# Squaring the recurrence's decay on VectorE instead of ScalarE, in a two-block layer stack

## The reference

```python
r = jax.nn.sigmoid(jnp.einsum('bsni,nij->bsnj', xb, w_a) + b_a).reshape(B, S, LRU_WIDTH)
i = jax.nn.sigmoid(jnp.einsum('bsni,nij->bsnj', xb, w_x) + b_x).reshape(B, S, LRU_WIDTH)
log_a = -LRU_C * r * jax.nn.softplus(-a_param)
a = jnp.where(reset, 0.0, jnp.exp(log_a))
mult = jnp.where(reset, 1.0, jnp.sqrt(-jnp.expm1(2.0 * log_a)))
b_in = xf * i * mult
_, h = lax.associative_scan(combine, (a, b_in), axis=1)      # h[t] = a[t] h[t-1] + b_in[t]
y = jax.nn.sigmoid(gate_a) * y_a + jax.nn.sigmoid(gate_b) * y_b
```

## Time and profile before

| What | Value |
|---|---|
| Median of three runs | 1880.51 us (1879.97 to 1885.79) |
| The profiled execution, its own time | 1880.51 us |
| Its span in the trace | 1878.7 us |
| TensorE busy | 1781.3 us, 95% of the span |
| VectorE, ScalarE, GpSimd busy | 976.1, 730.6 and 785.8 us |

### The profile page before, as it was taken

One profiled execution on the slowest core, in us unless ns is written; L12 is line 12 of the kernel. 1 busy time (PEld: TensorE's weight loads), 2 busy tenths in 40 slices (PEclk: granted clock), 3 DMA queues, 4 the chain that ended last, 5 costly groups with the idle time before them and its releaser, 6 DMA issues. The chain is left out here.

```text
span 1878.7 us, 23593 instructions
## 1 busy us (share of the span) xinstructions
PE 1781.3 (95%) x8447; PEld 1443.5 (77%) x8453; DVE 976.1 (52%) x1688; ACT 730.6 (39%) x1254; POOL 785.8 (42%) x363
## 2 busy tenths in 40 slices
PE   5987988999999999999999999999999999999997
PEld 4865867777888776878888888788776778888886
DVE  6989688748459977253324210559966131101112
ACT  4332365652357464232212222367554242222221
POOL 3345233325545520535445545355510544444442
PEclk9998999999999999999999999999999999999998
DMA  5433122206323310335555522233210222233311
GB/s 215 146 110 126 46 90 79 93 22 239 104 94 101 113 46 23 101 133 181 190 179 191 190 90 90 79 103 111 101 46 12 90 90 90 90 101 101 101 56 45
DMA packets 56057, 197.66 MB, mean 105 GB/s; under 512 B 6929, under 2 KB 7953, under 8 KB 55698
## 3 DMA queue, kind: packets, MB, share of 16 engines
q1 hardware_dynamic: 55954, 196.26, 31.0%
HBM read 194.14 MB, written 2.10 MB: 104 GB/s over the span
## 5 line engine op out<-in xcount | busy, mean ns | idle before, releaser
L458 POOL TENSOR_TENSOR WL<-RAW,WH 128x1024 fp32r<-128x1024 f32 x260 | 662.2, 2554 | 897.2 <-ACT WH L541 682.9
L1595 PE MATMUL bank<-HH,WH 128*128 128x512 f32 x1120 | 437.2, 390 | 6.6 <-POOLq L463 4.1
L1597 PE MATMUL bank<-HH,WL 128*128 128x512 f32 x1120 | 435.9, 389 | 0.0
L1596 PE MATMUL bank<-HL,WH 128*128 128x512 f32 x1120 | 435.8, 389 | 0.0
L541 ACT ACTIVATE WH<-RAW 128x1024 fp32r<-128x1024 f32 x260 | 271.3, 1051 | 261.0 <-PE bank L1597 235.0
L1595 PEld LDWEIGHTS bank<-HH,WH 128*128 128x128 f32 x1120 | 210.3, 188 | 52.7 <-issue 9.7
L1597 PEld LDWEIGHTS bank<-HH,WL 128*128 128x128 f32 x1120 | 210.3, 188 | 44.1
L1596 PEld LDWEIGHTS bank<-HL,WH 128*128 128x128 f32 x1120 | 210.3, 188 | 43.2
L1530 DVE TENSOR_TENSOR HF<-SILU,bank 128x512 f32<-128x512 f32 x44 | 30.3, 688 | 333.2 <-PE bank L1597 330.2
L1595 PE MATMUL bank<-HDH,WH 128*128 128x512 f32 x352 | 137.0, 389 | 0.0
L1597 PE MATMUL bank<-HDH,WL 128*128 128x512 f32 x352 | 136.9, 389 | 0.0
(11 more groups left out here) (336 smaller groups left out, 2943.3 us busy)
## 6 DMA issues: line engine op xcount, KB each, us to landing
RAW<-in_stream SPq DMA_DIRECT2D x364, 512.0 KB, 3.3
X<-in_xt SPq DMA_DIRECT2D x2, 1024.0 KB, 6.1
out_t<-YA SPq DMA_DIRECT2D x8, 256.0 KB, 2.2
ACC<-in_pos SPq DMA_DIRECT2D x1, 256.0 KB
gains<-in_gains SPq DMA_DIRECT2D x1, 224.0 KB
CS<-in_cs SPq DMA_DIRECT2D x1, 128.0 KB
cw<-in_cw SPq DMA_DIRECT2D x1, 128.0 KB
par<-in_par SPq DMA_DIRECT2D x1, 115.0 KB
```

The lines of the kernel that those rows point to most:

```text
L458: nc.gpsimd.tensor_tensor(lo(k)[:], raw(k)[:], hi(k)[:].bitcast(F32), ALU.subtract).then_inc(sem["passed"], mark("passed", *k))
L1595: nc.tensor.matmul(out, A[0], B[0], start=first, stop=False)
L1596: nc.tensor.matmul(out, A[0], B[1], start=False, stop=False)
L1597: return nc.tensor.matmul(out, A[1], B[0], start=False, stop=last)
```

## The change

Per layer, ScalarE's 8 Square instructions and their semaphore go. `one_aa(n)` on VectorE now waits for the Exp itself, multiplies LR[n] by itself into YT[n % 2], waits for that result, and then does the same (a^2 + 1) times YA as before, reading YT. The wait of the sigmoid of ga(4) for `one_aa(3)`, which protected SG[4] to SG[7], goes too. So does the tensor AA.

```diff
@@ -744,10 +739,6 @@
                         act.wait_ge(sem["tanh"], value("tanh", L, n))
                         nc.scalar.activation(LR[:, n, :], LR[:, n, :], ACT.Exp, scale=csc[:, L, n:n + 1]).then_inc(
                             sem["lru_a"], mark("lru_a", L, n))
-                    for n in ns:
-                        act.wait_ge(sem["lru_a"], value("lru_a", L, n))
-                        nc.scalar.activation(decay_square(n), LR[:, n, :], ACT.Square).then_inc(
-                            sem["lru_aa"], mark("lru_aa", L, n))
 
                 def roots(ns):
 
@@ -767,8 +758,6 @@
                             sem["xc_hi"], mark("xc_hi", L, n))
                     for n in GA_BESIDE[q]:
                         split_through(("ga", L, n))
-                        if n == 4:
-                            act.wait_ge(sem["one_aa"], value("one_aa", L, 3))
                         evict(SG[:, n, :], "ga", L, n, func=ACT.Sigmoid)
                     split_through(("lg", L, q))
                     for n in (2 * q, 2 * q + 1):
@@ -1415,8 +1404,10 @@
 
                 def one_aa(n):
 
-                    dve.wait_ge(sem["lru_aa"], value("lru_aa", L, n))
-                    V.scalar_tensor_tensor(out=YA[:, n, :], in0=decay_square(n), scalar=1.0, in1=YA[:, n, :],
+                    dve.wait_ge(sem["lru_a"], value("lru_a", L, n))
+                    V.tensor_tensor(YT[:, n % 2, :], LR[:, n, :], LR[:, n, :], ALU.mult).then_inc(step, 1)
+                    dve.wait_ge(step, own())
+                    V.scalar_tensor_tensor(out=YA[:, n, :], in0=YT[:, n % 2, :], scalar=1.0, in1=YA[:, n, :],
                                            op0=ALU.add, op1=ALU.mult).then_inc(
                         sem["one_aa"], mark("one_aa", L, n))
 
```

More of the change, by code:

```diff
@@ L166 @@
     "read_act", "full", "ca", "read_dve", "gmix", "h_hi", "lru_par", "lru_w", "topk", "iscore", "cos_sin",
-    "cmp_shift", "cmp_exp", "nmax", "mix_hi", "x_new", "conv", "xc_hi", "tanh", "lru_a", "lru_aa", "one_aa", "mult",
+    "cmp_shift", "cmp_exp", "nmax", "mix_hi", "x_new", "conv", "xc_hi", "tanh", "lru_a", "one_aa", "mult",
     "ya_gated", "c_hi", "y_full", "y_hi", "hid", "hid_hi", "x_half", "h_lo", "yb", "y_lo", "cmp_p", "xc_lo",
@@ L312, in program @@
         XCL = w("XCL", [P, 2, S], F32R, 84)
-        AA = w("AA", [P, 4, S], F32, 80)
         V2 = w("V2", [P, NT, D], F32, 32)
@@ L387, in spread @@
             return ap.rearrange(dims, o=1).broadcast_to(shape)
-        def decay_square(n):
-            return SG[:, 4 + n, :] if n < 4 else AA[:, n - 4, :]
         block = ctx.enter_context(nc.Block())
```

## The result

The changed kernel takes 1893.45 us, the median of seven runs (1890.62 to 1898.97). The kernel before takes 1883.12 us in the seven runs beside them (1879.97 to 1885.79). The ratio is 1.0057 with an interval of 1.0042 to 1.0073, so the change makes the kernel slower by 0.4 to 0.7%. The direction was predicted. The time lies 0.45 us above the end of the predicted range. The profiled execution took 1893.11 us. A ratio is worked out from all the runs of both kernels, and so it can differ by some hundredths of a per cent from the quotient of the two medians. Two runs in a slow state are in no median and no ratio of this document: one of the kernel before (7348.35 us) and one of e5_before_early (2393.78 us).

A forecast was written before the change was run, and what follows sets the result against it. TensorE, busy 95% of the span, was taken as the bound, with `one_aa(7)` delaying it one for one. 1880.5 + 5.8 (2 x 2.89, two layers) + 1.1 (one clock fall) = 1887.4 us, range 1881.9 to 1893.0.

The forecast's parts named there:

- the falls of the clock: TensorE's clock lowered behind the new stall at gb(3): 1.7 us gross, 1.1 net each, one counted for two layers.
- the starting time: Time of the kernel before that the sum starts from: 1880.5 us, the profiled execution and also the median.
- The pairs: Each added VectorE multiply, followed at once by the instruction needing its result: 0.71 us, 2.84 us for a group of four.
- the first group: Multiplies of tiles 0 to 3: covered by conv(5) starting 1.33 us early and a shorter XCL lock wait; 0.05 us left.
- What bounds the stage: Recurrence stage: what delays `one_aa(7)` delays TensorE at gb(3) one for one; making it earlier gives back only 0.2 us.
- the lock wait of XCL: XCL after conv(6), held by GpSimd's subtraction for 1.6 us before; it takes in 1.5 us of the first group's lateness.
- the cover: What hides the first four multiplies: 1.33 us gained at conv(5) and XCL's lock wait; without both, up to 2.84 us.
- the walk: Step-by-step timing of tiles 0 to 3 in the second layer, from the earlier copy to XCL after conv(6).
- The second group: Multiplies of tiles 4 to 7: full cost of 2.84 us; with 0.05 from the first group, gb(3) starts 2.89 us late.
- The twins above: Pauses near the end of attention in both layers: the second layer's clock fell to 0.57, the first's stayed at 1.00.
- the sum of 1888.5 us: Rival: clock falls at both stalls, 1.1 us more; the forecast with zero, one or two falls together had 0.62.

The follow-up runs named there:

- e5_before_early: Kernel before, with the WH copies for gb(3) and gb(4) made ahead of the second `roots`; 1886.30 us, ratio 1.0013.
- e6_twice: Changed kernel with each multiply of tiles 4 to 7 made twice; 1902.19 us, ratio 1.0092 to the kernel before.
- e1_first: Kernel before with only tiles 0 to 3 squared on VectorE, tiles 4 to 7 on ScalarE; 1885.45 us, ratio 1.0008.
- e7_kept: Kernel before with tiles 0 to 3 multiplied on VectorE while all eight Squares stay on ScalarE, the first four unused; 1887.11 us, ratio 1.0019.
- e3_fill: Changed kernel with fourteen unused bf16 matmuls on TensorE ahead of gb(3); 1889.30 us, ratio 1.0030 to the kernel before.
- e2_second: Kernel before with only tiles 4 to 7 squared on VectorE, tiles 0 to 3 on ScalarE; 1892.37 us, ratio 1.0046.
- a2_again: Changed kernel measured once more, without edit; 1891.27 us, ratio 1.0035 to the kernel before.
- e8_order: e5_before_early with the sigmoid of gb(7) moved behind the evictions of CQ and CK; 1878.87 us, ratio 0.9983 to the kernel before.

## Why the prediction was wrong, and what of it held

The forecast was 1887.4 us and the measured time 1893.45, 6.05 us more. Where TensorE would wait and why was right. Two terms of the sum were not: the falls of the clock, one counted where two came (1.2 us), and the starting time (2.6 us). The pairs and the first group make 0.3 us, and the other 1.9 us lie outside the stages.

**What bounds the stage: right.** The critical place is the matmul of gb(3), and `one_aa(7)` passes its lateness on one for one. It waits 3.30 us (forecast 3.1), and e6_twice adds 2.91 us for four multiplies. The removed Squares are worth nothing at that place, since ScalarE waits there 9.46 us (forecast 9.3).

**The first group: right, step by step.** Taking 8.53 us off VectorE's timeline, conv(5) starts at 1263.02 (forecast 1263.03), `one_aa(0)`'s multiply at 1270.91 (1270.90), conv(6) at 1278.43 (1278.36) and conv(7) at 1283.08 (1283.0). Of the lateness of 1.58 us at conv(6), 1.42 went into the lock wait of XCL, which took 0.87 us after 2.30. e1_first prices what is left at 0.14 us, for 0.05 forecast, and e7_kept shows that the earlier copy is the first half of the cover: without it 1.45 us arrive at gb(3), while XCL still takes in 1.4. One thing in this group was not in the walk and cancelled out. The first multiply took 2.89 us, held under the subtraction from 1279.27 to 1281.78, in place of the `one_aa` that was held there before. Both inputs of that multiply are the same tile, and it was held like an operation with two. The Trainium skill, SBUF — State Buffer, section "Who interferes with whom", says that a VectorE instruction with two SBUF inputs contends with a GpSimd instruction that reads SBUF. The trace agrees, with 2.89 against 0.68 us without a subtraction, and adds that one tile given twice counts as two inputs.

**The second group: right, 0.16 us a layer short.** The forecast was 2.89 us a layer and the distance to gb(3) gives 3.05. The pair takes 0.72 us instead of 0.71 (1324.98 to 1325.70), and VectorE enters the group 0.20 us late, where 0.05 was forecast.

**The clock: the mechanism right, the count wrong.** A fall behind gb(3) was put at 1.7 us gross and 1.1 net, and both figures were measured: 3.4 us at the lower level, and 1.17 us between gb(3) and uqr, which e3_fill takes away by filling the pause. The step that failed is "Each of two stalls may bring one. The twins above fell once in two, so I count one". The two twins of the earlier trace rows were pauses in thin work at the end of attention, and I carried their half over to a single pause in dense work. Even that half was read from one profile: in the three of the changed kernel both twins fell, six times of six. At gb(3) the clock fell behind all ten pauses of 3.16 us or more (the changed kernel three times, e2_second and e6_twice, two layers each) and behind none of the six of 1.22 us or less (before, e1_first and e7_kept). This term was 2.3 us and not 1.1. Between 1.22 and 3.16 us no run has a pause at gb(3), and at uqr one of 2.25 us brought a fall in one layer of two. The Trainium skill, TensorE: Matmul & The Clock Gate, Part 1, says that an idle array is gated to 1.2 GHz. The trace agrees, at both stalls, and this was the sum of 1888.5 us that the prediction gave as a rival.

**The sum of the stages.** Both stages together lose 4.16 + 4.22 = 8.4 us, where 6.9 was forecast: 1.2 from the second fall and 0.3 from the pairs and the first group. 8.4 us on 1883.1 is a ratio of 1.0045, which the interval of each of the three comparisons of the changed kernel holds (1.0057, 1.0035, 1.0060).

**The starting point: mis-sized, and with no spread.** The forecast started from 1880.5 us, the median of three runs. With 7 to 22 runs it is 1883.12, 1884.10, 1883.85 and 1882.67. On 1883.12 the same sum gives 1890.0 us and the range ends at 1895.6, above the result. So the miss of 0.45 us at the end of the range hangs on this term, and would hang on the second fall as well, since either one is more than 0.45 us, and the scatter of the starting time was not in the range at all.

**What stays open.** The three ratios have a mean of 1.0051, about 9.5 us, and the stages explain 8.4. In the first profile the changed kernel was already 2.51 us behind at conv(4) of the first layer. That shift goes with the clock's falls ahead of it, 20.5 to 29.0 us of full clock in the first 500 us over all profiles, where no changed instruction runs; a2_again, with as few as before, was 0.06 us behind there. Another part lies between the stages, from the first copy of KN in the first layer to conv(4) of the second. It took 586.04 us before and 587.90, 588.32 and 587.99 in the three profiles of the changed kernel, about 2 us more each time. All of them have two falls of 3.4 us in it, but not at the same places: before at 800.9 and 1179.8, changed at 756.6 to 761.5 and at 1193.5 to 1198.4. The first of these is the end of the first layer's attention, the twin that had stayed at 1.00 in the earlier trace rows. The stretch took 585.72 us in e8_order and 589.16 in e5_before_early, neither of which has an added multiply, so it changes without the change. Whether the 1 to 2 us beyond the 8.4 belong to it was not settled, with one profile of the kernel before.

## What to carry to other kernels

Before moving work to another engine, find the one place where the engine that bounds the kernel waits, and see which group of the moved instructions stands ahead of it: here eight of sixteen multiplies cost all of it and the other eight almost nothing. Price a new pause of TensorE in dense work as its length and, where it is as long as those that brought a fall here (3.16 us and more, not 1.22 and less), the fall of the clock, at every place where it stands, and take the starting time from as many runs as there are. Where an early copy only moves the wait, ask for the next place that depends on the same chain, since there a change of order (e8_order) is what helped.

## What was unexpected of the hardware

- A multiply of a tile with itself is held by a GpSimd subtraction like one of two tiles: 2.89 us for 0.68.
- The low clock at a pause came in two lengths: 3.4 us at pauses of 3.16 to 3.33 us, where it began behind the pause, and 6.8 us at those of 5.3 to 6.2, where it began inside. At a pause of 2.25 us it fell in one layer and not in the other (e5_before_early).
- The same instructions in the first 500 us missed between 20.5 and 29.0 us of full clock from one execution to another. That scatter of 8.5 us is as large as the effect of the change.
